# A trunk's first four weight tiles: three multiplied together for each pair of chunks of x, the fourth in halves

## What is computed

```python
def rmsnorm(x, g):
    y = x * rsqrt(mean(x * x, axis=-1) + EPS)
    return y * g

def swiglu(h, w_gate, w_up, w_down):
    return (silu(h @ w_gate) * (h @ w_up)) @ w_down

h = rmsnorm(x, ln_gains[0, 0])                 # x: 256 tokens x 1024
x = x + 0.5 * swiglu(h, w_gate[0, 0], w_up[0, 0], w_down[0, 0])   # d_ff = 2816
```

## Time and profile before

| | |
|---|---|
| median of three runs | 879.98 us (879.61 to 880.69) |
| the profiled execution | 881.48 us, its span 879.4 us |
| TensorE (PE) busy | 868.3 us, 99% |
| TensorE weight loads (PEld) | 764.5 us, 87% |
| DVE busy | 633.5 us, 72% |
| ACT busy | 467.7 us, 53% |
| loaded from HBM | 157.84 MB, 181 GB/s over the span |

### The profile page before, as it was taken

The page is one execution under the profiler, slowest core; times in us unless marked ns, Lnnn a source line. Parts: engine busy times, 40 slices in busy tenths (PEclk is TensorE's granted clock), DMA queues, the critical chain, the costliest instruction groups (busy, mean ns, idle before and its releaser), DMA issues.

```text
span 879.4 us, 12431 instructions
## 1 busy us (share of the span) xinstructions
PE 868.3 (99%) x5224; PEld 764.5 (87%) x5224; DVE 633.5 (72%) x728; ACT 467.7 (53%) x558; POOL 23.1 (3%) x49
## 2 busy tenths in 40 slices
PE   8999999999999999999999999999999999999997
PEld 7888888889999988888888888888888888888885
DVE  6997776668777698777666697776656998777452
ACT  6665555445555566555545375555544575555441
POOL 1000005300000000000000000000000000000000
PEclk9999999999999999999999999999999999999999
DMA  8686655565444438655556566655555277565431
GB/s 274 206 282 196 191 178 170 181 201 180 146 144 145 144 123 260 191 187 185 167 193 184 180 201 193 189 190 185 172 197 164 87 238 237 189 214 185 147 118 48
DMA packets 154167, 159.69 MB, mean 182 GB/s; under 512 B 2888, under 2 KB 152448, under 8 KB 154112
## 3 DMA queue, kind: packets, MB, share of 16 engines
q1 hardware_dynamic: 153760, 158.35, 56.4%
q10 hardware_dynamic: 352, 0.55, 0.2%
HBM read 157.84 MB, written 1.05 MB: 181 GB/s over the span
## 4 chain that ended last, share of the span: by engine, by line
PE 98%; DMA 1%; DVE 0%; ACT 0%; issue 0%; SPq 0%; DVEq 0%
PE psum L425 96%; PE psum L715 1%; PE psum L701 1%; DMA band<-in_x_dram 1%; PE psum L595 0%; PE psum L455 0%; ACT scratch L890 0%; DVE band L1151 0%; DVE h_all L1328 0%; DVE scratch L1154 0%; ACT h_all L975 0%; ACT soft L952 0%; DVE scratch L1349 0%; SPq L361 0%; SPq L359 0%
## 5 line engine op out<-in xcount | busy, mean ns | idle before, releaser
L425 PE MATMUL psum<-xg,w_hi 128*128 128x512 f32 (+1 forms) x1664 | 491.1, 380 | 0.0
L1011 DVE TENSOR_TENSOR w_lo<-raw,w_hi 128x2048 fp32r<-128x2048 f32 (+1 forms) x149 | 332.9, 2236 | 112.2 <-ACT w_hi L796 112.2
L425 PEld LDWEIGHTS psum<-xg,w_lo 128*128 128x128 f32 x1536 | 289.6, 189 | 62.7
L796 ACT ACTIVATE w_hi<-raw 128x2048 fp32r<-128x2048 f32 (+1 forms) x150 | 279.2, 1865 | 87.8 <-PE psum L425 87.4
L425 PE MATMUL psum<-xg,w_lo 128*128 128x256 f32 x1536 | 313.3, 279 | 0.0
L425 PEld LDWEIGHTS psum<-xg,w_hi 128*128 128x128 f32 x1664 | 255.0, 190 | 1.6 <-issue 0.7
L425 PE MATMUL psum<-h_all,w_hi 128*128 128x512 f32 (+1 forms) x656 | 189.4, 374 | 0.7 <-DVE h_all L1328 0.7
L425 PEld LDWEIGHTS psum<-h_all,w_lo 128*128 128x128 f32 x592 | 111.4, 188 | 23.4
L425 PE MATMUL psum<-h_all,w_lo 128*128 128x256 f32 x592 | 121.8, 278 | 0.0
L425 PEld LDWEIGHTS psum<-h_all,w_hi 128*128 128x128 f32 x656 | 100.3, 189 | 1.5 <-issue 1.5
L835 ACT ACTIVATE scratch<-psum 128x512 f32<-128x512 f32 x44 | 26.1, 593 | 84.9 <-PE psum L425 84.9
(11 more groups left out here) (114 smaller groups left out, 475.1 us busy)
## 6 DMA issues: line engine op xcount, KB each, us to landing
raw<-in_ffn_w_up_dram SPq DMA_DIRECT2D x43, 1024.0 KB, 5.3
raw<-in_ffn_w_gate_dram SPq DMA_DIRECT2D x42, 1024.0 KB, 5.3
raw<-in_ffn_w_down_dram SPq DMA_DIRECT2D x24, 1024.0 KB, 5.1
raw<-in_attn_w_qkv_dram SPq DMA_DIRECT2D x12, 1024.0 KB, 5.1
raw<-in_ffn_w_down_dram SPq DMA_DIRECT2D x20, 512.0 KB, 4.4
raw<-in_ffn_w_down_dram SPq DMA_DIRECT2D x12, 768.0 KB, 4.4
raw<-in_attn_w_o_dram SPq DMA_DIRECT2D x4, 1024.0 KB, 5.1
band<-in_x_dram SPq DMA_DIRECT2D x4, 256.0 KB, 5.1
```

Of the source, the lines that this page charges most:

```text
L425: return nc.tensor.matmul(out, stationary, moving, start=start, stop=stop, skip_group_check=True)
L796: nc.scalar.activation(w_hi[:, n % SPL, 0:size], raw[:, n % RAW, 0:size], ACT.Copy).then_inc(hi_split, 1)
L1011: nc.vector.tensor_tensor(w_lo[:, n % SPL, 0:size], raw[:, n % RAW, 0:size], w_hi[:, n % SPL, 0:size].bitcast(f32), ALU.subtract).then_inc ...
```

## The change

The first three tiles are worked on together. `STEPS` cuts the eight chunks of x into steps (0), (1), (2, 3), (4, 5), (6, 7). In each step x's columns are loaded, then tile 0's matching chunks and, from step 1 on, the matching pair of chunks of tiles 1 and 2 (step 1 takes chunks 0 and 1 of these). TensorE multiplies in the same order: tile 0's chunks of the step, then tile 1's, then tile 2's, into six banks (0 to 5). The transposes of the next step's x stand behind the first of tile 1's two chunks and go to banks 6 and 7 in turn, so `x_transposes` waits until DVE has copied the chunks of two steps before. The sums of squares are added after all of the split pieces, and the statistics stand before the last piece of tile 2. Tile 3 is loaded, split and waited for in halves. Its load waits for `lo_split` 1 as before, which is now counted when the last piece of tile 0 is split, in step 4. The statements on the semaphores and the removed waits are left out.

```diff
-    HALVED = 2
+    FIRST = 3
+    STEPS = ((0,), (1,), (2, 3), (4, 5), (6, 7))
+    PAIRS = ((0, 1), (2, 3), (4, 5), (6, 7))
...
+    def first_pieces(n):
+        return STEPS if n == 0 else PAIRS
+
+    def step_of(k):
+        return [s for s, ks in enumerate(STEPS) if k in ks][0]
+
+    def step_tiles(s):
+
+        return [(n, s if n == 0 else s - 1) for n in range(FIRST) if n == 0 or s]
...
+        def x_acc(d):
+
+            s = step_of(d)
+            at = STEPS[s].index(d) * SEQ
+            return psum[:, 6 + s % 2, at:at + SEQ]
...
-                        if n > HALVED:
+                        if n > FIRST:
                             load(n, cols, src[:, :, group])
-                        elif n > FFN0:
+                        elif n == FIRST:
+                            sp.wait_ge(lo_split, n - RAW + 1)
                             for half in range(2):
                                 ks = slice(half * DC // 2, (half + 1) * DC // 2)
-                                sp.dma_start(cols(raw[:, n, :])[:, ks, :], src[:, ks, group]) \
-                                  .then_inc(raw_loaded[n] if half else half_loaded[n - 1], 16)
-                    if n == HALVED + 1:
-                        sp.dma_start(late_rows[0:DC, :], pool_scale[0].rearrange("(c p) -> c p", p=P)) \
-                          .then_inc(late_loaded, 16)
+                                sp.dma_start(cols(raw[:, n % RAW, :])[:, ks, :], src[:, ks, group]) \
+                                  .then_inc(raw_loaded[n % RAW] if half else half_loaded, 16)
...
-            for c in range(DB):
-                pair = slice(c * GW, (c + 1) * GW)
-                sp.dma_start(x_tok[:, :, pair], x_v[:, :, pair]).then_inc(x_loaded[c], 16)
-                ks = slice(2 * c, 2 * c + 2)
-                sp.dma_start(cols(raw[:, 0, :])[:, ks, :], gate_v[0, 0][:, ks, 0:GW]) \
-                  .then_inc(piece_loaded[c] if c < DB - 1 else raw_loaded[0], 16)
+            first_src = (gate_v[0, 0][:, :, 0:GW], up_v[0, 0][:, :, 0:GW], gate_v[0, 0][:, :, GW:2 * GW])
+            for s, chunks in enumerate(STEPS):
+                x_cols = slice(chunks[0] * P, (chunks[-1] + 1) * P)
+                sp.dma_start(x_tok[:, :, x_cols], x_v[:, :, x_cols]).then_inc(x_loaded[s], 16)
+                for n, i in step_tiles(s):
+                    piece = first_pieces(n)[i]
+                    ks = slice(piece[0], piece[-1] + 1)
+                    sp.dma_start(cols(raw[:, n, :])[:, ks, :], first_src[n][:, ks, :]) \
+                      .then_inc(raw_loaded[n] if i == len(first_pieces(n)) - 1 else first_loaded[n][i], 16)
+            sp.dma_start(late_rows[0:DC, :], pool_scale[0].rearrange("(c p) -> c p", p=P)).then_inc(late_loaded, 16)
...
-                        if j == 0 and side == 0:
-                            if norm == 0 and k in (1, 3):
-                                x_transposes(k // 2 + 2)
+                        if j == 0 and side == 0 or n < FIRST:
                             pe.wait_ge(xg_lo_done, norm * DC + k + 1)
-                        if n == FFN0:
-                            if k < DC - 2:
-                                pe.wait_ge(piece_lo, k // 2 + 1)
-                            else:
-                                pe.wait_ge(lo_split, 1)
-                        elif n <= HALVED and k == 0:
-                            pe.wait_ge(half_lo, n)
+                        if n == FIRST and k == 0:
+                            pe.wait_ge(half_lo, 1)
                         elif n == FFN3 + 1 and k == 0:
                             pe.wait_ge(up_half, 1)
-                        elif (n <= HALVED or n == FFN3 + 1) and k == DC // 2:
+                        elif n in (FIRST, FFN3 + 1) and k == DC // 2:
...
-                    column_chunks(0, 0, range(DC))
-                    column_chunks(0, 1, range(DC))
-
-                    pe.wait_ge(x_done, DC // 2)
-                    column_chunks(1, 0, range(DC // 2))
-                    pe.wait_ge(x_done, DC)
-                    statistics(norm)
-                    pe.wait_ge(late_loaded, 16)
-                    nc.tensor.transpose(psum[:, stats_bank(0), SEQ:SEQ + DC], late_rows[:, :],
-                                        ident[0:DC, 0:DC]).then_inc(late_T, 1)
-                    column_chunks(1, 0, range(DC // 2, DC))
-                    weights(n0 + 3)
+                    for s in range(len(STEPS)):
+                        for n, i in step_tiles(s):
+                            piece = first_pieces(n)[i]
+                            if n == 2 and s == len(STEPS) - 1:
+
+                                pe.wait_ge(x_done, DC)
+                                statistics(norm)
+                                pe.wait_ge(late_loaded, 16)
+                                nc.tensor.transpose(psum[:, stats_bank(0), SEQ:SEQ + DC], late_rows[:, :],
+                                                    ident[0:DC, 0:DC]).then_inc(late_T, 1)
+                            if i < len(first_pieces(n)) - 1:
+                                pe.wait_ge(first_lo[n], i + 1)
+                            else:
+                                weights(n)
+                            column_chunks(n // 2, n % 2, piece[0:1])
+                            if n == 1 and s < len(STEPS) - 1:
+                                x_transposes(s + 1)
+                            column_chunks(n // 2, n % 2, piece[1:])
 
                     pe.wait_ge(newton, 1)
                     column_chunks(1, 1, range(DC))
...
-            def x_transposes(c):
-                pe.wait_ge(x_loaded[c], 16)
-                for d in (2 * c, 2 * c + 1):
+            def x_transposes(s):
+                pe.wait_ge(x_loaded[s], 16)
+                if s > 1:
+
+                    pe.wait_ge(x_done, STEPS[s - 2][-1] + 1)
+                for d in STEPS[s]:
                     for t in range(TT):
-                        last = nc.tensor.transpose(y_acc(d)[:, t * P:(t + 1) * P], x_tok[:, t, d * P:(d + 1) * P],
+                        last = nc.tensor.transpose(x_acc(d)[:, t * P:(t + 1) * P], x_tok[:, t, d * P:(d + 1) * P],
                                                    ident[:, :])
-                last.then_inc(x_T if c < DB - 1 else x_T_last, 1)
+                last.then_inc(x_T, 1)
...
-            idle_transposes(8)
+            idle_transposes(6)
...
             x_transposes(1)
-            idle_transposes(2)
+            idle_transposes(1)
...
-            for c in range(DB):
-                act.wait_ge(piece_loaded[c] if c < DB - 1 else raw_loaded[0], 16)
-                piece = slice(2 * c * GW, (2 * c + 2) * GW)
-                nc.scalar.activation(w_hi[:, 0, piece], raw[:, 0, piece],
-                                     ACT.Copy).then_inc(piece_hi if c < DB - 1 else hi_split, 1)
-                if c == 0:
-                    act.wait_ge(gains_done, 1)
-                round_chunk(0, 2 * c)
-                round_chunk(0, 2 * c + 1)
-
-            def split_hi_half(n, half):
-                act.wait_ge(raw_loaded[n] if half else half_loaded[n - 1], 16)
+            act.wait_ge(gains_done, 1)
+            for s, chunks in enumerate(STEPS):
+                for d in chunks:
+                    round_chunk(0, d)
+                for n, i in step_tiles(s):
+                    final = i == len(first_pieces(n)) - 1
+                    act.wait_ge(raw_loaded[n] if final else first_loaded[n][i], 16)
+                    piece = slice(first_pieces(n)[i][0] * GW, (first_pieces(n)[i][-1] + 1) * GW)
+                    nc.scalar.activation(w_hi[:, n, piece], raw[:, n, piece],
+                                         ACT.Copy).then_inc(hi_split if final else first_hi[n], 1)
+                if s > 1:
+                    square_x(0, s - 2)
+            square_x(0, DB - 1)
+            for half in range(2):
+                if half:
+                    act.wait_ge(raw_loaded[FIRST % RAW], 16 * loads(FIRST))
+                else:
+                    act.wait_ge(half_loaded, 16)
                 part = slice(half * ROWS // 2, (half + 1) * ROWS // 2)
-                nc.scalar.activation(w_hi[:, n, part], raw[:, n, part], ACT.Copy).then_inc(hi_split if half else half_hi, 1)
-
-            split_hi_half(1, 0)
-            split_hi_half(1, 1)
-            square_x(0, 0)
-            square_x(0, 1)
-            split_hi_half(2, 0)
-            square_x(0, 2)
-            square_x(0, 3)
-            split_hi_half(2, 1)
-            split_hi(3)
+                nc.scalar.activation(w_hi[:, FIRST, part], raw[:, FIRST % RAW, part],
+                                     ACT.Copy).then_inc(hi_split if half else half_hi, 1)
...
-            for c in range(DB):
-                piece = slice(2 * c * GW, (2 * c + 2) * GW)
-                if c < DB - 1:
-                    dve.wait_ge(piece_hi, c + 1)
+            for s, chunks in enumerate(STEPS):
+                for d in chunks:
+                    rest_chunk(0, d)
```

(77 more changed lines are left out.)

2 lines of the change are left out of this document (removed).

## The result

The changed kernel takes 886.88 us (median of six runs, 886.38 to 887.47), the kernel before beside it 880.28 us: a ratio of 1.0074, 95% interval 1.0061 to 1.0086, 6.6 us slower. The profiled execution took 887.35 us with a span of 885.3, against 881.48 and 879.4 before: 5.9 us in the spans.

The account below looks back on a forecast made before the run. TensorE's matmuls were taken to bound the kernel, any delay adding whole. The terms -0.9 + 1.4 + 1.6 + 2.05 + 1.1 gave +5.3 us (+5.4 worked in order of time), so 885.4 us, range 883.0 to 887.0.

Parts of the forecast that it names:

- (c): Head loads: pieces land late, a MB more coming 2 us later; 886.4 us, chance 0.12.
- (d): Start: single-chunk pieces land no sooner, nothing starts earlier, the 0.9 us gain is lost; 886.3 us, chance 0.05.
- The start, -0.9 in all: TensorE's first chunk 2.3 us earlier, less 1.1 for the lower clock and 0.3 for four later transposes.
- rival (a): TensorE's head: clock rises at 8.0 instead of 11.4 us; +3.9 us, 883.9 us, chance 0.27.
- Transposes, +1.4: Steps 2 to 4: TensorE waits after the moved x transposes, 0.35 + 0.54 + 0.54 us.
- Statistics, +1.6: Before tile 2's last piece: TensorE waits from 26.5 to 28.1 us for the sum of squares.
- Tile 3, +2.05: Before tile 3: its load waits for tile 0's slot, issued at 23.7 instead of 12.8 us; TensorE waits 2.05 us.
- The two layers: Wait before tile 3: even with tile 3 there in time, DVE's own queue would leave 0.65 us.
- Tile 5, +1.1: Before tile 5: DVE's chain from the mean to tile 5's low part comes 1.1 us late.
- Rival (b): First steps: DVE runs ahead, waits are covered, the start's 0.9 us gain stands; 879.1 us, chance 0.05.

Follow-up runs that it names:

- b_start: Kernel before with only the new start: x and tile 0 in pieces of one, one, two, two, two chunks; 881.35 us, ratio 1.0004.
- a_early_T: Changed kernel with the next step's x transposes behind the first chunk of tile 0 instead of tile 1; 884.19 us, ratio 1.0042.
- a_adds: Changed kernel with DVE's first add of squares moved ahead of step 4's rests; 886.47 us, ratio 1.0061.
- a_tile3: Changed kernel with tile 3 loaded early into unused parts of two buffers, not waiting for tile 0's slot; 884.67 us, ratio 1.0049.
- a_again: Changed kernel, unchanged, run again on another chip; 886.03 us, ratio 1.0062.
- third set: Last group of runs, on its own chip: changed kernel unchanged, with tile 5's load held back, and kernel before unchanged; the unchanged changed kernel's ratio 1.0062.
- a_load5: Changed kernel with tile 5's load issued only when tile 4 has landed; 886.10 us, ratio 1.0056.
- a_all: Changed kernel with three edits: x transposes earlier, tile 3 loaded early, first add of squares moved; 881.3 us, ratio 1.0004.
- a_all5: Changed kernel with transposes earlier, tile 3 loaded early, one add moved, and tile 5 split early by ACT and DVE; 880.27 us, ratio 0.9993.
- b_idle8: Kernel before with eight instead of two idle transposes behind the first x transposes; 879.62 us, ratio 0.9993.

## Why the prediction was right, point by point

885.4 us was forecast with a range of 883.0 to 887.0, and 886.88 measured, close to the upper end. Rivals (c) and (d), at 886.4 and 886.3, lie nearer to that number than the forecast does; it is the trace, with its waits in the places that the forecast named, that decides for the forecast. The terms it had are all there, one wait was missing, and several sizes were off, in both directions. The costs add up to 7.7 us where the sum had 6.15, and the gain at the start is 1.85 us (2.05 less the rest of 0.2) where it had 0.9. That these two errors of 1.6 and 0.95 us partly cancel is luck; together they turn the sum's 5.3 into the 5.9 of the spans.

- *The start, -0.9 in all*: the first chunk came 2.05 us earlier where 2.3 was put, since the trace of before starts at 7.91 and that of after at 5.86. But the 1.1 us that the forecast took off for the lower clock did not arise. It kept the rise at 11.4; in the profile after it came at about 9 us, so that the stretch at the lower clock is as long as before (5.86 to about 9 against 7.91 to 11.47). In this part rival (a) was true. b_start shows that the early start brings nothing as long as the chunks behind can't follow.
- *Transposes, +1.4*: measured +1.84. The mechanism is shown by a_early_T. Of the difference, 0.3 are the 0.10 us at the chunk behind each wait; the prediction had no such term, and the seven waits make 0.7 us of it.
- *Statistics, +1.6*: +1.80.
- *Tile 3, +2.05*: only +1.55. The issue came at 22.96, 0.8 us before the 23.8 reckoned, and the landing with it. The two layers are shown by a_adds (the sum earlier, the wait moved, no time gained) and a_tile3 (a remainder of 0.17 in the bracket, 0.44 from start to start, where 0.65 was put).
- *Tile 4, no term*: +0.63 in the profiled execution. This is the step that was missing. The loads of tiles 3, 4 and 5 are all issued within 2 us, and tile 4 lands 9.0 us after its issue, so ACT splits it at 33.26 and DVE at 35.21, after the wait for the mean is long over. In a_again it landed after 7.4 us and there was no wait, so the missing term is there in some executions and not in others.
- *Tile 5, +1.1*: +1.90, as tile 4's late split holds DVE up. In the execution with a landing of 7.4 us it was 0.56 of idle time, 0.8 from start to start, a little under the forecast.
- *Spans and medians*: the spans differ by 5.9 and the medians by 6.6, because the profiled execution of before took 1.2 us more than its median (881.48 against 880.28) and that of after 0.5 more (887.35 against 886.88). In the third set the two kernels' ratio is 1.0062, 5.5 us, so the size of the effect is itself known to about 1 us only.

Rival (b) did not occur, but a_early_T and a_tile3 bear out its mechanism: freed from TensorE's order and from the slot, DVE does run ahead, and the waits shrink. (d) did not, with the start at 5.86. (c) did not in this profile, where the only waits of the steps are those behind the transposes; in the profile of a_load5, whose head is the same, the first piece of tile 1 came later, and TensorE waited 0.32 us for it at 9.01.

## What to carry to other kernels

On an engine that works its list in order, a small step on which others wait (here four transposes) belongs as far ahead of its users as their chain is long; half a microsecond too late cost 0.6 us three times, and moving the transposes two chunks ahead removed it. Interleaving several tiles ends them all at nearly the same time, and their buffers come free together: ask what the slot of the first of them fed, and count the loads that then start together. And a wait that is removed pays only if it is the last layer; moving the add gained nothing until tile 3's load was out of the way.

## What was not expected of the hardware

- A wait of TensorE costs more than the idle time shown: a bracket of 0.34 us stood for 0.51 from start to start, and the next chunk took 0.80 instead of 0.70 us. A chunk right behind transposes took 0.79 without a wait.
- The rise of TensorE's clock falls at different times in executions of the same head: in the kernel before at 11.4 and between 9.2 and 9.9 us; in a_all and a_all5, which have the same head, after 9.4 and before 5.9 us. Six idle transposes more or nine fewer made no difference to the median that the intervals can tell.
- Transposes alone can bring the rise: in b_idle8 and a_all5 the clock was at its full level before the first matmul of the products.
- Tile 4's load of 1 MB landed 5.3 to 5.4 us after its issue in the kernels with tile 3 loaded early, with another 1 MB issued 0.6 us behind it. Behind tile 3's 1 MB it landed after 7.2 to 7.6 us in some executions and 8.9 to 9.0 in others, at the same order of issues.
